# Two elementwise products of the RWKV preparation: VectorE to GpSimd, fifteen interleaved steps for seventeen

## What is computed

```python
w_log = -jax.nn.softplus(-(w0 + jnp.tanh(wl) @ w2)) - 0.5
decay = jnp.exp(-jnp.exp(w_log))
a = jax.nn.sigmoid(a0 + al @ a2)
kk = hd(k * k_k)
kk = kk / jnp.maximum(jnp.sqrt(jnp.sum(kk * kk, axis=-1, keepdims=True)), 1e-12)
k = k * (1.0 + (a - 1.0) * k_a)
xs = tuple(jnp.moveaxis(t, 1, 0) for t in (r_h, w_h, k_h, v_h, -kk, kk * a_h))
S, y = lax.scan(wkv_step, S0, xs)     # S = S * w + (S a) b + v k,  y = S r,  with a = -kk, b = kk * a_h
bonus = jnp.sum(r_h * k_h * r_k, axis=-1, keepdims=True) * v_h
```

## Time and profile before

| | us |
|---|---|
| median of 3 runs (lowest, highest) | 1513.98 (1509.17, 1517.31) |
| the profiled execution's own time | 1510.73 |
| its span, first to last instruction | 1509.0 |
| PE busy in the span | 1402.4 |
| DVE busy in the span | 438.2 |
| POOL busy in the span | 110.0 |
| mean granted TensorE clock | 0.969 |

### The profile page before, as it was taken

How to read it: one execution, slowest core, us unless ns; L and a number is a source line. 1 busy time by engine, 2 the same in 40 slices (tenths; PEclk the granted TensorE clock), 3 DMA queues, 4 the chain that set the end, 5 groups by cost and what they waited for, 6 DMA issues and landing times.

```text
span 1509.0 us, 27895 instructions
## 1 busy us (share of the span) xinstructions
PE 1402.4 (93%) x11595; PEld 953.3 (63%) x11595; DVE 438.2 (29%) x917; ACT 357.0 (24%) x713; POOL 110.0 (7%) x223
## 2 busy tenths in 40 slices
PE   5999999988799999999989779999999999999997
PEld 4755666655577777777755454477777777744442
DVE  5022355455844444444445241310000000000002
ACT  3010233245444343443433331100000000000011
POOL 6283000000000000001202010000000000000000
PEclk9999899998799999999989889999999999999998
DMA  5187011023898787878957897003111221150001
GB/s 206 57 189 205 7 57 35 1 75 110 284 312 277 229 292 247 294 255 266 272 191 261 315 314 245 1 13 100 56 56 56 89 79 56 56 195 0 0 0 63
DMA packets 123174, 219.32 MB, mean 145 GB/s; under 512 B 11451, under 2 KB 35078, under 8 KB 123046
## 3 DMA queue, kind: packets, MB, share of 16 engines
q1 hardware_dynamic: 115154, 193.64, 38.3%
q0 software_dynamic: 7824, 23.85, 5.9%
q10 hardware_dynamic: 68, 0.02, 0.0%
HBM read 203.06 MB, written 14.41 MB: 144 GB/s over the span
## 4 chain that ended last, share of the span: by engine, by line
PE 84%; DVE 5%; DMA 4%; ACT 3%; issue 2%; SPq 1%; POOL 0%; DVEq 0%; POOLq 0%; ACTq 0%
PE PS L1369 23%; PE PS L736 13%; PE PS L1388 10%; PE PS L1178 6%; PE PS L1192 4%; PE PS L1308 4%; PE PS L1237 4%; PE PS L709 2%; DMA arena<-in_cache_k 2%; DMA out_wkv_prompt<-arena 1%; PE PS L1394 1%; PE PS L992 1%; PE PS L1002 1%; PE PS L996 1%; ACT arena L1622 1%
## 5 line engine op out<-in xcount | busy, mean ns | idle before, releaser
L1369 PE MATMUL PS<-arena 128*128 128x288 f32 x1408 | 342.1, 405 | 1.2 <-DVE arena L2251 1.2
L1369 PEld LDWEIGHTS PS<-arena 128*128 128x128 f32 x1408 | 265.7, 189 | 77.4 <-DVE arena L2251 1.4
L736 PE MATMUL PS<-arena 128*128 128x301 f32 (+1 forms) x736 | 197.7, 426 | 0.0
L1622 ACT ACTIVATE arena<-PS 128x512 f32<-128x512 f32 x256 | 141.4, 596 | 192.8 <-PE PS L1178 192.4
L1178 PE MATMUL PS<-arena 128*128 128x128 f32 x1024 | 153.8, 296 | 27.1 <-DMA arena<-in_cache_k 15.1
L736 PEld LDWEIGHTS PS<-arena 128*128 128x128 f32 (+1 forms) x736 | 136.6, 189 | 54.7 <-issue 13.6
L1178 PEld LDWEIGHTS PS<-arena 128*128 128x128 f32 x1024 | 122.1, 151 | 55.8 <-issue 24.2
L1388 PE MATMUL PS<-arena 128*128 128x512 f32 x352 | 151.5, 592 | 1.5 <-DVE arena L2277 1.5
L1388 PEld LDWEIGHTS PS<-arena 128*128 128x128 f32 x352 | 66.5, 189 | 86.2 <-issue 84.3
L2277 DVE TENSOR_TENSOR arena<-PS,arena 128x576 f32<-128x576 f32 x22 | 16.7, 758 | 327.0 <-ACT arena L1686 327.0
L1686 ACT ACTIVATE arena<-PS 128x576 f32<-128x576 f32 x22 | 14.3, 651 | 329.8 <-PE PS L1369 329.8
(11 more groups left out here) (360 smaller groups left out, 1409.9 us busy)
## 6 DMA issues: line engine op xcount, KB each, us to landing
arena<-in_cache_k SPq DMA_DIRECT2D x256, 256.0 KB, 4.3
arena<-in_cache_v SPq DMA_DIRECT2D x256, 256.0 KB, 4.8
arena<-in_w_gate SPq DMA_DIRECT2D x11, 1024.0 KB
arena<-in_w_up SPq DMA_DIRECT2D x11, 1024.0 KB
arena<-in_w_in SPq DMA_DIRECT2D x5, 2048.0 KB, 11.9
forgets_after<-arena POOLq DMA_DIRECT2D x64, 128.0 KB, 8.5
arena<-forgets_after SPq DMA_DIRECT2D x32, 256.0 KB, 5.1
arena<-in_w_down SPq DMA_DIRECT2D x4, 2048.0 KB
```

What stands on the lines that cost most here:

```text
L736: ins = mm(PS[0:width, bank, 0:HALF], wring[:, c % 2, k, c0:c0 + width], xnT[:, k, half * HALF:(half + 1) * HALF], start=(k == 0), stop=(k ...
L1369: ins = mm(PS[:, 4 * (f % 2) + 2 * w + half, 0:HO], fring[r % FR][:, c:c + P], hT[:, k, half * HO:(half + 1) * HO], start=(k == 0), stop=( ...
L1622: av(KTs[:, (2 * i + q) % LOT], PS[:, T_USE[("k", L, i, q)] % 2, :].rearrange("p (g n) -> p g n", g=NG), ACT.Copy)\
```

## The change

DVE's products of lines 1913 and 1921 go to POOL, in place, with the same operands. POOL issues them behind the load of `g2`. The first waits for `hs_taken` 4 (the keys are normalised) and for `rate_read`, which each of the four instructions of line 1902 now raises when it has read `Bd`; the second for the first and for `decays` 3; it raises `ab_ready`. DVE waits for `ab_ready` ahead of the product of line 1926, which overwrites `Kd`. N_PRE goes from 17 to 15: DVE's list loses the two steps, PE's two of its six empty steps, ACT's two of its seven. `ab_ready` and `rate_read` take the places of two semaphores that nothing waits for.

```diff
-        N_PRE = 17
+        N_PRE = 15
...
             pool.dma_start(G2, t_in["g2"][0]).then_inc(S["g2_in"], 16)
+            pool.wait_ge(S["hs_taken"], 4)
+            pool.wait_ge(S["rate_read"], NG)
+            ch(g.tensor_tensor(Bd, Bd, kk, ALU.mult))
+            pool.wait_ge(S["decays"], 3)
+            g.tensor_tensor(Bd, Bd, Kd, ALU.mult).then_inc(S["ab_ready"], 1)
             pool.wait_ge(S["pre_done"], 1)
...
                 low_rank(7)
                 yield
-                for _ in range(6):
+                for _ in range(4):
                     yield
...
-                for _ in range(7):
+                for _ in range(5):
                     yield
...
-            ins.then_inc(S["qb_ready"], 1)
...
                 for g in range(NG):
-                    ch(ts(T2[:, g], Bd[:, g], -1.0, pc("k_a", g), ALU.add, ALU.mult))
-                yield
-                ch.wait()
+                    ts(T2[:, g], Bd[:, g], -1.0, pc("k_a", g), ALU.add, ALU.mult).then_inc(S["rate_read"], 1)
+                yield
+                dve.wait_ge(S["rate_read"], NG)
                 ch(stt(XR[:, 4:8], T2, 1.0, XR[:, 4:8], ALU.add, ALU.mult))
...
                 dve.wait_ge(S["decays"], 3)
-                ch(tt(Bd, Bd, kk, ALU.mult))
-                yield
                 ch(stt(AR[:, 0], kk, -1.0, AR[:, 0], ALU.mult, ALU.mult))
...
                 ch.wait()
-                ch(tt(Bd, Bd, Kd, ALU.mult))
-                yield
                 ch(tt(AR[:, 1], XR[:, 0:4], AR[:, 1], ALU.mult))
                 yield
                 ch.wait()
+                dve.wait_ge(S["ab_ready"], 1)
                 ch(tt(Kd, XR[:, 4:8], Kd, ALU.mult))
```

More of the change, by code:

```diff
@@ L185, in build @@
         ncb_ready ncb_taken s_ready s_added mx_ready exp_done p_ready pt_ready pt_taken pv_ready o_taken out_done
-        qb_ready kts_ready act_c dve_c pool_c pt_zero shn_turned shn_ready
+        ab_ready kts_ready act_c dve_c pool_c pt_zero shn_turned shn_ready
         lr_in lr_act lr_ready lr_taken hs_in hs_ready hs_rows hs_taken pre_done L_ready decays root_in root_done
@@ L191, in build @@
         fs_taken fs_out yc_ready rwkv_done prev_tile
-        k_free v_free wo_in x2_in gu_ready down_used ln_in y_final
+        k_free v_free wo_in x2_in gu_ready rate_read ln_in y_final
         kt_taken sc_taken sc_page nm_ready exp_out pr_turned pr_taken ov_ready ov_taken new_ready nmn_ready expn_out
```

## The result

The change makes the kernel slower by one per cent: 1527.85 us in the median of 7 runs against 1513.53 for the kernel before, ratio 1.0104 with a 95% interval of 1.0082 to 1.0126. The profiled execution took 1523.6 us, 12.9 more than that of before.

What follows compares the result with a forecast made beforehand. PE was busy for 93% of the span, but DVE could be on the path in the preparation. Order, +2 alone, with POOL disturbing DVE made +7 in all; added to the median 1513.98 this gave 1521 us, range 1510 to 1527.

Steps and rivals of the forecast that it cites:

- two forms of disturbance: In the preparation, POOL's products slow DVE by whole-instruction waits, +8.7, or halving, +6.5; taken as +7, chance 0.62.
- part three: POOL's two products take 5.63 us each, with 3.5 us of cover before DVE waits for `ab_ready`.
- part four: What POOL's products do to DVE while both run in the preparation: between +2 and +8.7, taken as +7 with the order.
- the first bound: In the preparation, a DVE instruction waits for the whole POOL instruction; +8.7 us with the order included.
- the gentler ones: In the preparation, both engines halved while they overlap, +6.5, or no disturbance, +2, the latter with chance 0.20.
- The selects beside the scans: POOL's selects took 329 ns beside DVE's two-input scans, 292 afterwards; read as a sign of little disturbance.
- part two: The order of fifteen steps instead of seventeen costs the preparation +2 us, if POOL disturbs nobody.
- the wait for keys: PE's wait before the keys of lot 2 grows from 3.98 to about 5.5 us: +1.5.
- the new wait before tile 0: PE, through with piece 26, waits 2.3 us before line 962 for the preparation to end.
- the one that hurts: Step 8 moves from behind piece 12 to behind piece 13, delaying the keys of lot 2 by about 1.5 us.
- DVE's relief: Two products leave DVE's queue; at most 4.98 us of PE's waits return directly. Rival that it makes the kernel faster: 0.10.
- The later steps: The 123 steps after the preparation meet lots up to three pieces earlier; nothing in the sum, 4 us allowed either way.

Runs made afterwards that it cites:

- e3: The change with both products left out on any engine, fifteen steps kept; 1522.17 us, ratio 1.0063 to the kernel before.
- e1: The change with products on POOL but all seventeen steps kept, two of them empty on DVE; 1520.74 us, ratio 1.0052 to the kernel before.
- e5: The change with seventeen steps, products left out and POOL running memsets that only write in their place; 1510.53 us, ratio 0.9983 to the kernel before.
- e6: The change with seventeen steps and each POOL product cut into four parts of 640 columns; 1515.11 us, ratio 1.0020 to the kernel before.
- e2: The kernel before with both products left out on any engine, seventeen steps kept; 1511.88 us, ratio 0.9996.
- e7: The kernel before with SP issuing the keys of lot 2 ahead of the bias of lot 1; 1510.55 us, ratio 0.9988.
- e8: The change with SP issuing the keys of lot 2 ahead of the bias of lot 1; 1526.30 us, ratio 1.0110 to the kernel before.
- e9: The change with steps 1 to 8 and all tile steps behind their old pieces; 1522.69 us, ratio 1.0056 to the kernel before.
- e12: The change with products back on DVE, steps 1 to 8 and all tile steps behind their old pieces; 1521.48 us, ratio 1.0075 to the kernel before.
- e4: The change with the products back on DVE, fifteen steps kept; 1526.66 us, ratio 1.0101 to the kernel before.
- e10: The kernel before with DVE's bonus of groups 0 and 1 ahead of the product for Kd; 1508.76 us, ratio 0.9985.

## Why the prediction was wrong

The forecast was 1521 with 1510 to 1527; the median is 1527.85, just above, and the increase twice what I forecast (14.3 against 7).

Two terms of the sum were too small, and they are the steps that failed. For the preparation I took +7, a value between two forms of disturbance, and it lost 9.0 in the trace. For the tiles I took nothing, with 4 either way, and they lost 3.9. That makes the 12.9 us between the two profiled executions; the 1.4 more between the medians lie in the spread of executions, and no trace places them.

- *POOL's products* (part three): 5.61 and 5.59 us against 5.63, starts at 379.50 and 388.63 against 379.3 and 388.6. Right, and the cover ahead of `ab_ready` held: no run of DVE waited there.
- *DVE and POOL at once* (part four): the end I called the first bound was the truth, on DVE nearly to the tenth. Line 1905's product ended at 387.80, worked out as 385.0 + 2.8; line 1909's at 397.3 against 397.6; PE's wait was 6.02 against 6.2; line 962 came at 418.27 against the 419.8 that is in +8.7. The step that failed was taking a value between this end and the gentler ones. That the whole preparation lost 9.0, so near to 8.7, is in part luck: the bound was +2 for the order and +6.7 for the exclusion, the runs give 4.9 for the order without products (e3) and 6.5 for POOL alone (e1), and these do not add. The selects beside the scans misled me; they are lengths of POOL's instructions, and in the change it was DVE that was held. e5 and e6 confirm the rule of the Trainium skill ("SBUF — State Buffer", Who interferes with whom) for exactly this pair: DVE with two SBUF inputs, POOL reading, one instruction at a time; a POOL instruction that only writes leaves DVE alone., where a memset held a one-input `tensor_scalar` of DVE, is another case: the same section of the Trainium skill names `tensor_scalar` among the instructions that can enter VectorE's two-port modes and then contend with GpSimd. No run here shows in which mode line 1713 ran.
- *The order* (part two): I gave it +2 in the preparation. Without products and without POOL it costs 4.9 (e3), and 7.1 against the same kernel in seventeen steps (e2), by the two lags that need care. Of its terms, the wait for keys grew as said, 5.29 against 5.5, and the new wait before tile 0 is 2.00 against 2.3. But I added waits along one engine as if each were on the path. The keys alone are not: with their wait taken away no gain can be told (e7, e8), another wait takes the place. And with the eighth step back in its old place the preparation loses as much (e9, e12), so its delay, which I called the one that hurts, is not what costs. What hurts, as I read the traces of e4 and e12, is that two steps fewer take three pieces of PE's cover out of a chain that keeps its length: there PE waits 7.4 and 8.5 us before the second bonus sums.
- *DVE's relief* (what bounds the kernel): "at most 4.98 us" was an upper bound, and the truth is 2.2 in the trace and nothing that the medians can tell (e2, 0.9976 to 1.0015). The 3.78 us wait was named DVE's by the profile, which is correct, but it hangs on the order of DVE's list, as e10 shows.
- *The later steps*: I gave them 4 us either way. They cost 3.9 in the change, still inside that, and 4.4 to 8.2 in three other runs with the same shift; what failed is that the sum went by nothing for them; e9 and e12, which undo the shift, show -0.7 and -2.4. This is the term that carried the result out of my range: the 9.0 of the preparation alone would have stayed in it. Why the shift costs and does not gain I can only guess: the list had been laid out for one meeting of lots and tiles. Only this one shift was run.

What stays open: why PE stood for 2.6 us of "issue" at line 1017, which no engine's signal explains. It is no accident of one execution: the other three runs with shifted tiles stop before the same matmul of PE's list for 1.3 to 2.3 us, and no other run stops there. And I have not resolved the two parts of the preparation's loss when both causes act. They overlap; I suppose that DVE held by POOL and DVE's products in one row both make PE wait for the same chain once, and no run shows it.

## What to carry to other kernels

Before moving work from VectorE to GpSimd, list what VectorE does during the move: if it has products of two SBUF operands there and GpSimd's instruction reads SBUF too, moving 2.8 us of its work can stop it for longer than that, here for 5.3 (8.15 against 2.82). In a hand-interleaved schedule a step is not overhead to be saved but a slot for the other stream's cover; taking two out cost more here than the collision (14.2 us in the medians against 8.3). And to learn what an engine's relief is worth, leave its work out for one run (e2): that took one kernel and would have stopped this change.

## What the runs showed of the hardware that I had not expected

In these runs the engine that starts first keeps the other out until its instruction ends, in both directions: a DVE product of one column took 1.48 us instead of 0.16 beside a POOL part of 640 columns, and four POOL parts took 10.03 us instead of 5.6 when DVE got in between (e6). The instructions of DVE that were held read two operands in SBUF: line 2108, which reads one, began 0.53 us into POOL's second product and kept its 0.15 us. A DVE instruction that is held counts as busy in the profile. That is why DVE's busy time rose by 4.4 us with two products less: 10.1 us of being held against 5.65 us of products moved. A busy share can hide a wait.
